# GpSimd subtracts a weight tile in pieces of 256 columns instead of in one instruction

## What is computed

```python
h = rms(x, norm1_g);  proj = h @ w_in
o_a = rwkv(...); o_b = sliding_window_attention(...); o_m = cross_attention(...)
br = einsum('btnc,ncd->btnd', stack([o_a, o_b, o_m]), w_branch)
x = x + sum(sigmoid(gates) * br) @ w_out
h = rms(x, norm2_g)
a_in, u = split(h @ w_up)                      # 2 x 2816 columns
c = conv_b + causal_depthwise_conv3(a_in)
x = x + (gelu(c) * u) @ w_down
```

## Time and profile before

| | |
|---|---|
| median of 3 runs | 2286.06 us (2284.76 to 2289.59) |
| profiled execution, its own time | 2281.92 us |
| span of that execution, first to last instruction | 2280.1 us |
| TensorE matmul busy | 2142.4 us, 94% |
| GpSimd busy | 1144.9 us, 50% |
| VectorE busy | 969.9 us, 43% |
| ScalarE busy | 902.3 us, 40% |
| granted TensorE clock, mean | 0.977 |
| DMA | 243.83 MB, mean 107 GB/s |

### The profile page before, as it was taken

One profiled execution on the slowest core, in us unless ns is written; L12 is line 12 of the kernel. 1 busy time (PEld: TensorE's weight loads), 2 busy tenths in 40 slices (PEclk: granted clock), 3 DMA queues, 4 the chain that ended last, 5 costly groups with the idle time before them and its releaser, 6 DMA issues.

```text
span 2280.1 us, 41379 instructions
## 1 busy us (share of the span) xinstructions
PE 2142.4 (94%) x17511; PEld 2021.2 (89%) x17511; DVE 969.9 (43%) x1655; ACT 902.3 (40%) x1450; POOL 1144.9 (50%) x694
## 2 busy tenths in 40 slices
PE   4899899999999999979999999999898999998899
PEld 4799699899999999969989999999887898988899
DVE  4454733454444323483335444431446434544430
ACT  4444333335444433532333444442443333454432
POOL 2534333365676553333335576756333433667775
PEclk9989899999999999989999999999998999999999
DMA  4422122243434452211124333355321212544344
GB/s 144 125 93 75 43 57 61 76 157 117 124 120 149 142 167 75 69 62 57 50 79 137 127 120 121 122 163 178 109 75 56 67 52 88 168 130 126 124 138 136
DMA packets 85960, 243.83 MB, mean 107 GB/s; under 512 B 11024, under 2 KB 24592, under 8 KB 85776
## 3 DMA queue, kind: packets, MB, share of 16 engines
q1 hardware_dynamic: 85776, 241.18, 33.9%
HBM read 235.06 MB, written 6.09 MB: 106 GB/s over the span
## 4 chain that ended last, share of the span: by engine, by line
PE 77%; DVE 7%; POOL 5%; issue 4%; ACT 4%; DMA 2%; SPq 1%; DVEq 0%; ACTq 0%; POOLq 0%
PE sums L300 20%; PE sums L301 19%; PE sums L302 19%; PE px L1438 5%; POOL w_lo L424 4%; PE ps_o L1015 2%; ACT w_hi L318 2%; PE px L1451 1%; PE pp L1384 1%; POOL gl L448 1%; PE ps_t L992 1%; PE ps_x L944 1%; PE pz L1714 1%; SPq L802 1%; DMA raw<-w_attn 1%
## 5 line engine op out<-in xcount | busy, mean ns | idle before, releaser
L424 POOL TENSOR_TENSOR w_lo<-raw,w_hi 128x1024 fp32r<-128x1024 f32 (+1 forms) x452 | 1008.2, 2235 | 982.1 <-ACT w_hi L318 981.9
L300 PE MATMUL sums<-x_hi,w_hi 128*128 128x384 f32 (+1 forms) x2208 | 753.8, 341 | 53.1 <-DVE h L541 25.9
L301 PE MATMUL sums<-x_lo,w_hi 128*128 128x384 f32 (+1 forms) x2208 | 727.6, 330 | 0.0
L302 PE MATMUL sums<-x_hi,w_lo 128*128 128x384 f32 (+1 forms) x2208 | 727.4, 329 | 0.0
L318 ACT ACTIVATE w_hi<-raw 128x1024 fp32r<-128x1024 f32 (+1 forms) x452 | 437.8, 971 | 245.3 <-PE sums L302 74.5
L300 PEld LDWEIGHTS sums<-x_hi,w_hi 128*128 128x128 f32 x2208 | 420.7, 191 | 88.5 <-issue 64.8
L301 PEld LDWEIGHTS sums<-x_lo,w_hi 128*128 128x128 f32 x2208 | 421.5, 191 | 2.4
L302 PEld LDWEIGHTS sums<-x_hi,w_lo 128*128 128x128 f32 x2208 | 420.7, 191 | 0.0
L300 PE MATMUL sums<-h_hi,w_hi 128*128 128x384 f32 (+1 forms) x528 | 172.5, 327 | 0.0
L302 PE MATMUL sums<-h_hi,w_lo 128*128 128x384 f32 (+1 forms) x528 | 172.0, 326 | 0.0
L301 PE MATMUL sums<-h_lo,w_hi 128*128 128x384 f32 (+1 forms) x528 | 172.0, 326 | 0.0
(11 more groups left out here) (310 smaller groups left out, 2808.4 us busy)
## 6 DMA issues: line engine op xcount, KB each, us to landing
raw<-w_up SPq DMA_DIRECT2D x132, 512.0 KB, 3.6
raw<-w_gate SPq DMA_DIRECT2D x72, 512.0 KB, 3.6
raw<-w_down SPq DMA_DIRECT2D x48, 512.0 KB, 3.7
raw<-w_rwkv SPq DMA_DIRECT2D x42, 512.0 KB, 3.6
raw<-w_branch SPq DMA_DIRECT2D x72, 256.0 KB, 2.7
raw<-w_attn SPq DMA_DIRECT2D x30, 512.0 KB, 3.9
raw<-w_out SPq DMA_DIRECT2D x24, 512.0 KB, 3.5
raw<-w_down_end SPq DMA_DIRECT2D x24, 384.0 KB, 3.0
```

What stands on the lines that cost most here:

```text
L300: pe.matmul(out, wh[:, ws], n.hi[:, k, :], start=(n.begins and k == 0), stop=False)
L301: pe.matmul(out, wh[:, ws], n.lo[:, k, :], start=False, stop=False)
L302: mm = pe.matmul(out, wl[:, ws], n.hi[:, k, :], start=False, stop=(n.ends and k == n.kt - 1))
L424: pool.tensor_tensor(lo_of(c, u), raw_of(c, u), hi_of(c, u).bitcast(F32), ALU.subtract).then_inc(S["w_lo_pool"], 1)
```

## The change

`split` in `dense_pool` no longer subtracts the tile in one instruction. It goes through the tile in pieces of 256 columns: four instructions for a tile of 1024 columns, three for 768, two for 512. All pieces stand directly behind each other in GpSimd's queue, behind the same one wait for w_hi, and only the last raises the semaphore `w_lo_pool`, so its count stays as it was. Operands, results and all other engines' programs are unchanged.

```diff
+PIECE = 256
...
     def split(u):
         if u < len(c.units) and c.units[u].splitter == "pool":
             pool.wait_ge(S["w_hi"], u + 1)
-            pool.tensor_tensor(lo_of(c, u), raw_of(c, u), hi_of(c, u).bitcast(F32), ALU.subtract).then_inc(S["w_lo_pool"], 1)
+            lo, raw, hi = lo_of(c, u), raw_of(c, u), hi_of(c, u).bitcast(F32)
+            for at in range(0, c.units[u].kt * P, PIECE):
+                cols = slice(at, at + PIECE)
+                ins = pool.tensor_tensor(lo[:, cols], raw[:, cols], hi[:, cols], ALU.subtract)
+            ins.then_inc(S["w_lo_pool"], 1)
```

## The result

| | before | after |
|---|---|---|
| median | 2286.74 us (2283.46 to 2289.59, 8 runs) | 2297.23 us (2293.42 to 2302.42, 8 runs) |
| profiled execution, its own time | 2281.92 us | 2302.42 us |
| its span | 2280.1 us | 2300.6 us |
| granted TensorE clock, mean | 0.977 | 0.973 |

The changed kernel is slower: ratio 1.0041, 95% interval 1.0029 to 1.0054, or 10.5 us between the medians.

What follows compares the result with a forecast made beforehand. TensorE was taken as bounded in the up stage by a closed loop through VectorE, GpSimd and ScalarE. Terms 1.7 + 8 + 3.4 + 3.0 - 3.6 - 1.8 = +10.7 us gave 2297 us, range 2264 to 2318.

Steps and rivals of the forecast that it cites:

- The price of a piece: GpSimd's w_lo subtraction: each instruction costs 0.16 us whatever its width, so a full tile in four pieces costs +0.48 us.
- rival (c): A piece costs less than 0.16 us, its start hidden behind its predecessor; about -8 us, 2278 us; chance 0.10.
- Who gets in between: VectorE and GpSimd take turns by instruction, so h_lo goes in between pieces and shrinks from 1.53 to about 0.6 us.
- Rival (b): GpSimd keeps the operands until its last piece, so h_lo waits for all four; about +68 us, 2354 us; chance 0.09.
- The small copy: Up stage, VectorE: the two-column copy L528 is held by piece 3, so a_raw starts 0.44 us earlier in the first groups.
- rival (a): Two-column copies are not held by GpSimd, so the up-stage turn shrinks by 0.40 to 0.45 us; -20, 2266 us; chance 0.16.
- The loop of the first two groups: Up-stage chain of waits: 0.48 us lost on the first tile, 0.44 gained at a_raw; 42 turns of +0.04, +1.7 us.
- The loop of the last group: Up-stage chain where second copy L530 meets piece 4: 21 turns give +1.3 to +14.5 us, the middle, +8, taken.
- Fresh starts and last branches: Places where TensorE waits for w_lo itself: seven grow by 0.48 us (+3.4), four in the last branches by 0.75 (+3.0).
- The place that was costed at nothing: Outside the counted places, w_lo is two units ahead of TensorE and a 4.1 us unit hides the 0.48 us.
- Gains beside the recurrence: VectorE's b_n and k_n come 1.2 us earlier and g_y 0.6 us, three times each: -3.6 and -1.8 us.

Runs made afterwards that it cites:

- experiment with gl ahead: Tiles whole, GpSimd's gl step moved ahead of the coming tile's subtraction, against the kernel before: 2330.75 us beside 2288.39, ratio 1.0178.
- The parts by themselves: Pieces only in up units, attention/memory/recurrence projections, gate and branch units, or wo and wd, each against the kernel before: 0.9989, 1.0020, 0.9989, 0.9991.

## Why the prediction was right, and where only its sum was

The forecast was 2297 us, slower by 10.7 us than the kernel before, and 2297.2 was measured. The sum hit closer than its terms did.

**The price of a piece: right in kind, a little high.** 2.82 us was forecast for four pieces, and without a guest they take 2.80 us up to the next instruction. But the whole tile that they replace takes 2.38 us on this path, not 2.34, so the price is 0.42 us a tile and not 0.48, or 0.14 us for each instruction more. The other widths agree: two halves cost 0.14, eight pieces 0.99 (7 x 0.14). That is above the 0.10 at which rival (c) begins.

**Who gets in between: right.** h_lo was to shrink to about 0.6 us and lasts 0.49 to 0.57 in all 66 pairs of the up stages. Rival (b) didn't appear at this width.

**The small copy: right, and the loop hung on it.** L533 (before: L528) was to be held by piece 3 and last about 0.6 us; it lasts 0.70 in 63 of the 66 pairs, all but the first of each group. a_raw was to start at W + 2.36 and starts at W + 2.38. So rival (a), under which the change would have gained 20 us, falls. The Trainium skill, page "SBUF — State Buffer", section "Who interferes with whom", has the pair of engines shut each other out for whole instructions when a VectorE copy uses both ports. The rows agree, down to two columns, and the 2.35 us copy of the experiment with gl ahead shows it most plainly.

**The loop of the first two groups: right in mechanism, smaller in size.** +0.04 us a turn was forecast, from 0.48 lost and 0.44 gained. It was 0.42 and 0.42, and the turn stayed within 0.004 us; 42 turns give nothing instead of +1.7.

**The loop of the last group: the term that was too high.** The prediction had not been able to tell which of two instructions would win a meeting in the same hundredth, and took the middle, +8. The second copy wasn't held in any of the 22 pairs, and the mean turn is 8.381 us against 8.388. The term is -0.1 instead of +8. The middle was a price for not knowing, and a value that neither case gives. Also, 19 and not 21 of the 22 waits for h recur in the last group's loop: one is its first pair, and two are the first pairs of the other groups. In these three first pairs the change costs 0.4 us each, 1.2 us that the sum doesn't have.

**Fresh starts and last branches: too small.** 3.4 + 3.0 = 6.4 us of added waiting for w_lo was forecast; it is 36.8 - 20.0 = 16.8. The waits in the last branches of the last group went from 2.4 to 5.4 us, as forecast. The other seven grew by 5.1 instead of 3.4. The mv unit's wait, which stands under another line (L287) and wasn't counted, grew by 3.4. And 5.3 us are waits in eight places where TensorE had not waited for w_lo at all: 3.1 in the attention units ahead of mv, 0.3 behind it, 1.1 in the last branches of the first two groups, and 0.8 in w_down.

**The place that was costed at nothing: a term that was missing.** "Elsewhere w_lo is two units ahead" does not hold in the memory stage. VectorE normalises there in instructions of 1024 columns, and three tiles are due at once. Before, then after:
```profile
112.81 9.05 POOL L424 TENSOR_TENSOR w_lo<-raw,w_hi 128x1024 fp32r<-128x1024 f32 x3 [7.54 <-ACT w_hi L318]
...
113.07 3.26 DVE L107 SCALAR_TENSOR_TENSOR ar<-ar 128x1024 f32<-128x1024 f32 x1
116.37 3.27 DVE L109 SCALAR_TENSOR_TENSOR ar<-ar 128x1024 f32<-128x1024 f32 x1
```
```profile
115.79 11.32 POOL L428 TENSOR_TENSOR w_lo<-raw,w_hi 128x256 fp32r<-128x256 f32 x12 [7.13 <-ACT w_hi L319]
...
116.06 1.63 DVE L108 SCALAR_TENSOR_TENSOR ar<-ar 128x1024 f32<-128x1024 f32 x1
117.72 1.63 DVE L110 SCALAR_TENSOR_TENSOR ar<-ar 128x1024 f32<-128x1024 f32 x1
119.39 1.63 DVE L776 SCALAR_TENSOR_TENSOR mk<-mk,k_vecs,ar 128x1024 f32<-128x1024 f32 x1
```
VectorE's long instructions used to get in once a tile and now get in once a piece. They go from 3.26 to 1.63 us and are through early, which nobody needs. GpSimd's three tiles take 11.32 us instead of 9.05, and TensorE stands for them: 7.4 us instead of 4.0. The prediction weighed the turns from the guest's side, and from the host's only in the last branches. The host pays for each of them, and here the host was the one on the path.

**Gains beside the recurrence: right, and nearly all of it reached TensorE.** Three groups' b_n and k_n: from the start of a_r to the end of k_n 3.56 us instead of 4.64, -1.08 against -1.2 forecast. g_y: 0.97 us against 1.51, -0.54 of -0.6. The prediction missed r_y, which shrank from 2.58 to 0.97 in the same place; of it VectorE's next instructions give a good half back. From the start of r_t to the end of k_n, VectorE takes 16.20 us instead of 17.77 (260.78 to 276.98 against 253.40 to 271.17). TensorE's waits for r_y and k_n don't show the gain: together they are 25.8 us against 25.0. That is because TensorE's own work between the two waits got shorter. Before, then after, in the first group:
```profile
257.21 4.48 PE L1384 MATMUL pp<-r_y,k_from_rows 128*128 128x384 f32 x8 [2.95 <-DVE r_y L109]
...
271.22 1.98 PE L1451 MATMUL px<-a_r,b_n 64*64 64x128 f32 x32 [5.35 <-DVE k_n L1626]
...
273.99 0.53 PE L300 MATMUL sums<-o_hi,w_hi 128*128 128x384 f32 x1
274.35 0.34 PE L301 MATMUL sums<-o_lo,w_hi 128*128 128x384 f32 x1
```
```profile
262.99 2.85 PE L1389 MATMUL pp<-r_y,k_from_rows 128*128 128x384 f32 x8 [1.13 <-DVE r_y L110]
...
277.03 1.99 PE L1456 MATMUL px<-a_r,b_n 64*64 64x128 f32 x32 [7.01 <-DVE k_n L1631]
...
279.80 0.69 PE L301 MATMUL sums<-o_hi,w_hi 128*128 128x384 f32 x1
280.28 0.52 PE L302 MATMUL sums<-o_lo,w_hi 128*128 128x384 f32 x1
```
The eight matmuls behind the wait for r_y ran mostly at half clock before (granted 0.63 on average) and at full clock after, so TensorE came to the wait for k_n earlier and stood there for longer. Behind that wait the granted clock is 0.50 in both. Before, it is back after 3.0 us; after, only after 5.0 us (282.03), and five more matmuls take 0.52 us instead of 0.34, which costs 0.9 us. What counts is how long TensorE takes from its last matmul ahead of the wait for r_y (253.93, after the change 261.52) to the eighth dense matmul behind k_n (275.42 and 282.14): 20.62 us instead of 21.49, and in the other groups 20.45 instead of 21.51 and 19.45 instead of 20.98. Together 3.4 us are gained (3.3 in the second profile of the change), where 3.6 was forecast. The wait for rk, behind g_y, fell from 5.3 to 3.7 us, 1.6 of the 1.8 forecast.

**The sum.** The forecast put +8 on the last group's loop, which gave nothing, and 6.4 instead of 16.8 us on the waits for w_lo. The two errors nearly cancel, so that the time came out at the forecast is luck. The mechanisms of the loop and of the gains were right without it.

**What stays open.** The first measurement gives +10.5 us, the second +3.9 (2292.32 against 2288.39), and their intervals do not meet (1.0029 is the low end of the one, 1.0028 the high end of the other). The parts by themselves (0.9989, 1.0020, 0.9989, 0.9991) multiply to 0.9989, less than either. That it is slower is shown twice; whether by 0.15 or by 0.4% is not settled. All waits of TensorE add up to 132.9 us before, 149.6 after and 148.6 in the second profile of the change, so the waits grow by 16 us both times. TensorE's busy time doesn't repeat: for the same 17511 matmuls it is 2142.4 us before, 2146.6 after, 2137.6 in the second profile, and 2154.5 with pieces in the up units alone. It goes with the clock, and a good part of it lies in the attention stage of the last group. The same 867 matmuls and the waits between them, in the kernel before, the changed one, its second profile, and the one with pieces in the up units (stretch, its us, busy us and matmuls, granted clock, DMA):
```profile
1613.80:1754.20 140.40, 133.62 (x867) 0.93 0.24 72
1627.50:1774.40 146.90, 139.75 (x867) 0.88 0.22 69
1623.20:1764.10 140.90, 133.66 (x867) 0.93 0.23 72
1618.50:1765.80 147.30, 139.80 (x867) 0.88 0.22 69
```
The fourth kernel has its tiles whole there and takes as long as the second (6.9 and 6.5 us more than before). The third has them in pieces and takes only 0.5 us more. So about 6.5 of the 20.5 us between the two spans are not the pieces' doing. The medians carry such a share too. In the second measurement the changed kernel's 12 runs had a mean granted clock of 0.9764, the 23 runs of the kernel before 0.9743, and among those 23 a clock higher by 0.001 goes with a time shorter by 1.9 us. As an estimate, at equal clock the second measurement would give some +8 us. Whether the change itself moves the clock was not tested, and the rest of the gap to the 16 us of waits is open.

## What to carry to other kernels

Cutting an instruction lets in whoever waits for it and costs the one that is cut, so cut it only where the guest is on the path and the host is not: the same cut was worth -21.8 us on one tile of a pair, and on both the loop's turn didn't change. Look for it in the trace as an instruction that lasts two to three times its like and ends with a neighbour engine's; then ask separately for each place who stands behind the host. Before choosing the width, compare the time at which the guest asks with the pieces' borders, since with halves it missed its turn by 0.04 us, and with 128 columns it sometimes got none.

## What the hardware showed that I had not expected

- A copy of two columns waits for a running GpSimd subtraction like a wide one: 0.70 us behind a piece of 256 columns, 2.35 us behind a tile of 1024, 0.15 us without company.
- The order of turns isn't always one and one: with 128-column pieces h_lo was served in some turns (0.83 us) and stood to the end in others (2.48 to 2.53 us, once 5.04), in the same queues, at the same place of the loop. Ten of 66 were of the second kind. All 66 asked within 0.05 us of a border between pieces, some a little before and some a little behind it, and both kinds stand on either side. Which condition decides was not found.
- A longer stand of TensorE doesn't simply mean a longer stretch at half clock behind it. Behind the k_n waits of the three groups the clock stayed at half for 3.0, 3.3 and 4.0 us before (waits of 5.3 to 5.5 us), for 5.0, 4.3 and 2.8 us after (7.0 to 7.2 us), and for 4.8, 4.8 and 3.3 us in the second profile of the change. It is longer in two groups and shorter in the third. No run changed the wait alone.
